# A two-layer encoder on one core: phases that end with one barrier and without GpSimd's drain, on two sets of semaphores

## The chip, the cores and the metric

The kernel runs on one core of one Trainium2 chip. The metric is the device time of one execution in microseconds, smaller is better. A core has five engines with queues of their own: TensorE (PE; its weight loads are PEld), VectorE (DVE), ScalarE (ACT), GpSimd (POOL) and SyncE (SP), and 16 DMA engines that all of them share. Engines wait for each other on semaphores only. A name with a q behind it (POOLq, SPq) is the engine's sequencer, where drains, semaphore instructions and DMA issues are shown.

## The reference

What is computed is an encoder trunk of two layers on one sequence of 1024 tokens of width 1024, in float32. Cut to its structure:

```python
def reference(x, ...):
    for layer in range(2):
        hn = rms_norm(x, mix_norm[layer])
        if layer == 0:
            u = hn @ ev_w_in
            y_att = diff_attention(u[..., :1536], ...)   # 4 heads, two softmaxes subtracted
            y_hy = hyena_mixer(u[..., 1536:], ...)       # long convolution through an FFT
            y = concatenate([y_att, y_hy]) @ ev_w_out
        else:
            u = hn @ od_w_in
            y = mlstm_mixer(u, ...) @ od_w_out           # chunkwise scan, forward and backward
        x = x + y
        x = x + hier_moe(rms_norm(x, ffn_norm[layer]), ...)
    return x

def hier_moe(x, ...):
    # top 1 of 4 groups, then top 2 of 8 experts inside it; tokens sorted by expert,
    # padded to blocks of 128, each block through its expert:
    hid = silu(xe @ w1[e]) * (xe @ w3[e])
    y = hid @ w2[e]
    # rows scaled by their gates and summed back per token
```

## The kernel before, in words

The program is a chain of 13 phases, run strictly one behind the other. In order they are: the attention projection (block at line 243), attention (533), the Hyena projection (1330), the Hyena filter (1548), the Hyena transform (1703), output projection and router of layer 0 (811), the experts of layer 0 (1976), the values of the mLSTM (2411), its gates (2627), its queries and keys (2828), its scan (2965), output projection and router of layer 1 (811 again) and the experts of layer 1 (1976 again). One block behind these, at the end of `build`, is only built when phases are cut off, and is not part of the program here.

A phase is one `nc.Block`: in it each engine has its own instruction list, and within a phase engines meet on semaphores written out by hand. `take(n)` hands a phase its semaphores: the first n of one pool of 46. Every phase counts from zero on the same ones. Semaphores that live across phases (those of the weight ring, `chunk_in`; of the gathered rows, `gather_in`; of the scattered rows, `given`; and some more) are allocated beside the pool and never cleared.

When a block closes, every engine drains (waits for its own instructions) and all engines meet at a barrier; GpSimd's drain is among these. `end_phase` (lines 110 to 113) then runs `nc.all_engine_barrier(sems_to_clear=pool_range)`: a further drain of every engine, a meeting at GpSimd, the clear of the pool's 46 semaphores by GpSimd, and a release of all engines. A phase is thus followed by two barriers, and the next phase's first instruction comes behind both.

What crosses the seams: SP loads weights into a ring of three slots of 2 MB (`load_chunk`, line 172), always three chunks ahead; `refill` and the loops of the expert phase issue them as slots come free, so that the first chunks of a phase are issued in the phase before. The router phase ends with two indirect gathers by GpSimd (line 867), which fetch the rows of the first two experts into `xg`, and VectorE's gates of the slots (lines 1278 and 1279).

In an expert phase GpSimd issues the indirect DMAs: `fetch` gathers the rows of expert e (line 2035), `give` adds the results of expert e to the output rows (line 2050), one more gather for an overflow block (line 2068), and for each further overflow block a gather (2086) and an adding scatter (2094), of which layer 1 has one here and layer 0 none. Before its list ends GpSimd waits for the last of the `give` transfers (line 2077), for `put` (line 1933) and for the last gather (line 2100). ScalarE casts each weight half to its high part (line 2228, the phase's first ScalarE work), VectorE takes the rest (2292), TensorE transposes the gathered rows (2131) and multiplies (2114 to 2122).

The values phase behind the experts of layer 0 begins on SP with loads of the residual rows just written, `x_ml` from `x_scratch` (line 2418), a broadcast gain, and further rows. ScalarE squares the rows (line 2494), VectorE normalises them (2562), TensorE turns them (2440) and multiplies (206 to 208). TensorE starts with 44 filler products (`idle_products`, line 201) before the first turn.

In the Hyena transform GpSimd multiplies eight pieces of `yT` in place (line 1893, counted on `added`); in the scan it adds the backward results onto the forward ones (line 3085, counted on `added_ok`). Nothing in those phases waits for the last of these counts: the drain at the block's end covers them.

Of the kernel before, what the change touches and what calls it, by code (L numbers as in the profile page):

```python
# [76 lines left out]
def build(nc, I, out):  # L77
    ctx = ExitStack()
    with ctx:
        POOL = 46  # L80
        pool = [nc.alloc_semaphore(f"phase_sem{i}") for i in range(POOL)]
        pool_range = range(pool[0].num, pool[0].num + POOL)
        chunk_in = [nc.alloc_semaphore(f"chunk_in{i}") for i in range(RING)]
# [11 lines left out]
        phases = [0]  # L95
# [14 lines left out]
        def end_phase():  # L110

            nc.all_engine_barrier(sems_to_clear=pool_range)
            phases[0] += 1

        def sb(stack, name, shape, dt=F32, side=None):
            return stack.enter_context(nc.sbuf_tensor(name, shape, dt, side=side))
# [95 lines left out]
        def attention_project(q, kH, kL, v, src, gain):  # L212
# [5 lines left out]
            with ExitStack() as st:  # L218
# [23 lines left out]

                with nc.Block() as block:
                    @block.sync
# [265 lines left out]
        def attention(q, kH, kL, v, o):  # L510
            (scored, max_neg, expd, comb, turned_lo, turned_hi, wt_lo, wt_hi, summed, o_copied, lam_in, lam_ok,
             chain, q_high, q_rest) = take(15)
            with ExitStack() as st:
# [18 lines left out]

                with nc.Block() as block:
                    @block.sync
# [162 lines left out]
        def out_route(name, yT, hs, head_gain, s0, xsrc, xdst, layer, slots, slot_gate, ctrl, xg):  # L697
# [6 lines left out]
            with ExitStack() as st:  # L704
# [105 lines left out]

                with nc.Block() as block:
                    @block.sync
# [471 lines left out]
        def hyena_project(z, yT, xnH, o, gain, post, hidden, consts):  # L1284
# [4 lines left out]
            with ExitStack() as st:  # L1289
# [39 lines left out]

                with nc.Block() as block:  # L1330
                    @block.sync
# [204 lines left out]
        def hyena_filter(z, zT, hidden, consts, hs, hd, hinv, tab):  # L1536
# [4 lines left out]
            with ExitStack() as st:  # L1541
# [5 lines left out]
                SUM = 6  # L1547
                with nc.Block() as block:
                    @block.sync
# [105 lines left out]
        def hyena_transform(z, zT, both, tab, hinv, yT):  # L1655
# [4 lines left out]
            with ExitStack() as st:  # L1660
# [7 lines left out]
                UNITS = 2 * FT  # L1668
# [31 lines left out]
                def result_of(c, i):  # L1700
                    return (KR if c else G)[:, 2 * i:2 * i + 2, :]

                with nc.Block() as block:
                    @block.sync
                    def _(sp):
                        sp.dma_start(skip[:], I["hy_skip"]).then_inc(skip_in, 16)
                        sp.wait_ge(done, forward_order(1, 0) + 4)
                        for kt in range(FT):
                            sp.dma_start(both[:, 8 * kt:8 * kt + 8, 0:CH], I["c_idft"][kt]).then_inc(inv_in[kt], 16)
# [177 lines left out]
                    @block.gpsimd  # L1887
                    def _(pool_e):
                        for n in range(2 * 4):
                            c, i = divmod(n, 4)  # L1890
                            g = times(yT[:, 4 + 2 * c + i // 2, :], i % 2)
                            pool_e.wait_ge(scaled, n + 1)
                            nc.gpsimd.tensor_tensor(g, g, result_of(c, i), ALU.mult).then_inc(added, 1)
                end_phase()


        @phase
        def experts(layer, slots, slot_gate, ctrl, total, xg, y, yidx, oidx, w_over):
# [9 lines left out]
            with ExitStack() as st:  # L1908
# [66 lines left out]

                with nc.Block() as block:
                    @block.sync
# [374 lines left out]
                for c in range(3):  # L2352
                    n = s0 + 3 * NE + c
# [26 lines left out]
        def ml_values(vA, xnH, src, gain):  # L2380
# [4 lines left out]
            with ExitStack() as st:  # L2385
# [24 lines left out]

                with nc.Block() as block:
                    @block.sync
# [185 lines left out]
        def ml_gates(xnH, cols, colb, apr, so, qkH):  # L2598
# [5 lines left out]
            with ExitStack() as st:  # L2604
# [21 lines left out]

                with nc.Block() as block:
                    @block.sync
# [176 lines left out]
        def ml_project_qk(qkT, xnH, wH):  # L2805

            (proj, padded, convolved, silued, weights_in, edges, chain, w_high, w_rest, first_half, lower) = take(11)
            with ExitStack() as st:
# [18 lines left out]

                with nc.Block() as block:
                    @block.sync
# [101 lines left out]
        def ml_scan(qkT, kn, vA, cols, colb, apr, hs):  # L2931
# [3 lines left out]
            with ExitStack() as st:  # L2935
# [9 lines left out]
                UNITS = NT * 2 * MH  # L2945
# [5 lines left out]
                FIRST = UNITS // 2  # L2951
# [12 lines left out]

                with nc.Block() as block:
                    @block.sync
# [110 lines left out]
                    @block.gpsimd  # L3077
                    def _(pool_e):
                        def add(u):
                            c, d, h, gi, n, col = unit(u)  # L3080
                            dst = hs[:, n, h * MV:(h + 1) * MV]
                            if u == FIRST:
                                pool_e.wait_ge(h_ok, FIRST)
                            pool_e.wait_ge(scaled_ok, u - FIRST + 1)
                            nc.gpsimd.tensor_tensor(dst, dst, num[:, u % 4, 0:MV], ALU.add).then_inc(added_ok, 1)

                        pool_e.wait_ge(k_lo, NT // 2)
                        pool_e.wait_ge(k_hi, NT // 2)
                        for u in range(UNITS):
                            if u < STATED:  # L3090
                                c, d, h, gi, n, col = unit(u)
                                if u >= 2:
                                    pool_e.wait_ge(cc_ok, u - 1)
                                nc.gpsimd.tensor_scalar(kw[:, u % 2, :], kn[:, n, h * P:(h + 1) * P], col(3), None,
                                                        ALU.mult).then_inc(kw_ok, 1)
                            if u - 4 >= FIRST:
                                add(u - 4)
                        for u in range(UNITS - 4, UNITS):
                            add(u)

                    @block.vector
# [134 lines left out]
        if phases[0] >= LAST_PHASE[0]:  # L3236
            with nc.Block() as block:
                @block.sync
                def _(sp):
                    for n in range(RING):  # L3240
                        sp.wait_ge(chunk_in[n], 16 * issued[n])
# [107 lines left out]
```

## Time and profile before

| | us |
|---|---|
| median of 3 runs | 2589.49 (2587.01 to 2590.59) |
| profiled execution: span from first to last instruction | 2584.1 |
| profiled execution: a time of its own beside the span | none is shown |
| TensorE busy | 2384.6 (92%) |
| VectorE busy | 1817.3 (70%) |
| ScalarE busy | 1457.0 (56%) |
| GpSimd busy | 472.1 (18%) |
| instructions | 32457 |

The page of the profile gives the busy time of each engine over the whole span. Drains, semaphore instructions and DMA issues do not count as busy; they stand in the view by source line, with their durations and the time of the first and the last start. The timeline gives starts to a hundredth of a microsecond, with the idle time before an instruction and what ended it in square brackets. The DMA view of a stretch gives the busy share (in tenths) and the GB/s of the DMA engines in 40 equal columns.

### The profile page before, as it was taken

To read this page: it belongs to the slowest core of one execution; us is meant where nothing else is said; L and a number is where in the kernel's file an instruction comes from. 1 tells how busy PE (TensorE), PEld (TensorE's weight loads), DVE (VectorE), ACT (ScalarE), POOL (GpSimd) and SP (SyncE) were. 2 spreads that over 40 slices of the span, in tenths; PEclk is the share of its full clock that TensorE was granted. 3 is DMA by queue.
4 is the path that set the end of the run, shared out by engine and by line. 5 is a ranking of instruction groups with operands and counts; after the bars stand their busy time and mean duration, and the time that the engine had idled before them with its cause. 6 is when DMAs were issued, how large, how long until landed. Compare 5 with 4: busy or idle time off the path is not lost. (4 is left out here: it accounts for less than half of the span.)

```text
span 2584.1 us, 32457 instructions
## 1 busy us (share of the span) xinstructions
PE 2384.6 (92%) x11594; PEld 1956.3 (76%) x11594; DVE 1817.3 (70%) x2055; ACT 1457.0 (56%) x1782; POOL 472.1 (18%) x433
## 2 busy tenths in 40 slices
PE   8989999796978999999996999997997999999996
PEld 7768877485867888888885877875775888888884
DVE  7848856568457998989883141478647899888982
ACT  6438842322216787888873241267424788887881
POOL 0001100102002333333320000026001233332321
PEclk9999999898988999999998999999997999999998
DMA  5110011111337999999995022012435999999996
GB/s 180 53 48 2 2 41 45 73 33 30 114 130 272 380 393 371 390 388 382 385 379 201 17 95 102 33 50 76 166 128 208 376 374 383 370 395 380 392 386 238
DMA packets 94377, 546.55 MB, mean 212 GB/s; under 512 B 19260, under 2 KB 31133, under 8 KB 68294
## 3 DMA queue, kind: packets, MB, share of 16 engines
q1 hardware_dynamic: 72822, 507.16, 50.3%
q0 software_dynamic: 19008, 33.61, 5.4%
q10 hardware_dynamic: 2448, 4.46, 0.5%
q8 instruction: 62, 1.02, 0.2%
q14 instruction: 37, 0.30, 0.0%
HBM read 525.72 MB, written 55.08 MB: 225 GB/s over the span
## 5 line engine op out<-in xcount | busy, mean ns | idle before, releaser
L2292 DVE TENSOR_TENSOR wL<-ring,wH 128x2048 fp32r<-128x2048 f32 x384 | 869.4, 2288 | 135.4 <-ACT wH L2228 129.4
L2228 ACT CAST wH<-ring 128x2048 fp32r<-128x2048 f32 x384 | 729.9, 1911 | 200.4 <-DMA ring<-in_moe_w 147.6
L2114 PE MATMUL psum<-wH,xgH 128*128 128x512 f32 x1024 | 407.1, 398 | 13.1 <-DVE xgL L2292 13.1
L2116 PE MATMUL psum<-wH,xgL 128*128 128x512 f32 x1024 | 400.9, 392 | 0.0
L2122 PE MATMUL psum<-wL,xgH 128*128 128x512 f32 x1024 | 275.2, 391 | 0.0
L2114 PEld LDWEIGHTS psum<-wH,xgH 128*128 128x128 f32 x1024 | 193.5, 189 | 54.7 <-DVE xgL L2292 13.3
L2122 PEld LDWEIGHTS psum<-wL,xgH 128*128 128x128 f32 x1024 | 192.8, 188 | 40.5
L2116 PEld LDWEIGHTS psum<-wH,xgL 128*128 128x128 f32 x1024 | 193.6, 189 | 38.5
L2114 PE MATMUL psum<-wH,hidH 128*128 128x512 f32 x512 | 206.0, 402 | 3.4 <-DVE hidL L2292 3.4
L2116 PE MATMUL psum<-wH,hidL 128*128 128x512 f32 x512 | 200.2, 391 | 0.0
L2032 POOL COPY gidx<-slots 128x1 int32 (+1 forms) x60 | 58.1, 968 | 496.4 <-PE psum L2131 496.4
L2122 PE MATMUL psum<-wL,hidH 128*128 128x512 f32 x512 | 137.7, 391 | 0.0
L208 PE MATMUL psum<-xn_high,ring_rest 128*128 128x512 f32 x320 | 126.6, 396 | 0.0
L2114 PEld LDWEIGHTS psum<-wH,hidH 128*128 128x128 f32 x512 | 96.5, 189 | 22.6 <-DVE hidL L2292 3.8
L206 PE MATMUL psum<-w_high_route_rest,y_high_route 128*128 128x512 f32 x256 | 104.0, 406 | 9.4 <-DVE ring_rest L196 8.9
L2122 PEld LDWEIGHTS psum<-wL,hidH 128*128 128x128 f32 x512 | 96.7, 189 | 20.2
L2116 PEld LDWEIGHTS psum<-wH,hidL 128*128 128x128 f32 x512 | 96.7, 189 | 18.3
L208 PE MATMUL psum<-w_high_route_rest,y_rest_route 128*128 128x512 f32 x256 | 101.0, 394 | 0.0
L207 PE MATMUL psum<-ring_rest,y_high_route 128*128 128x512 f32 x256 | 100.9, 394 | 0.0
L207 PE MATMUL psum<-ring_rest,xn_high 128*128 128x512 f32 x256 | 100.8, 394 | 0.0
L2046 POOL COPY yidx<-slots 128x1 int32 (+1 forms) x64 | 88.0, 1374 | 64.6 <-DMA out<-y,yidx 33.4
L629 DVE TENSOR_REDUCE neg_max<-psum 128x1 f32<-128x1024 f32 x64 | 75.4, 1220 | 29.2 <-PE psum L553 29.2
(436 smaller groups left out, 4622.2 us busy)
## 6 DMA issues: line engine op xcount, KB each, us to landing
ring<-in_moe_w SPq DMA_DIRECT2D x192, 2048.0 KB, 9.5
ring<-in_ev_w_in SPq DMA_DIRECT2D x6, 2048.0 KB, 10.1
xnT<-in_moe_w SPq DMA_DIRECT2D x6, 2048.0 KB, 15.2
ring<-in_od_w_in SPq DMA_DIRECT2D x6, 2048.0 KB, 15.5
xn_scratch<-xn_route SPq DMA_DIRECT2D x16, 512.0 KB, 2.6
ow<-in_moe_w SPq DMA_DIRECT2D x3, 2048.0 KB, 24.0
v_att<-in_x SPq DMA_DIRECT2D x8, 512.0 KB, 4.5
ring<-in_ev_w_out SPq DMA_DIRECT2D x2, 2048.0 KB, 7.8
```

Of the source, the lines that this page charges most:

```text
L206: nc.tensor.matmul(dst, lhs[0], rhs[0], start=start, stop=False)
L207: nc.tensor.matmul(dst, lhs[0], rhs[1], start=False, stop=False)
L208: return nc.tensor.matmul(dst, lhs[1], rhs[0], start=False, stop=stop)
L629: nc.vector.tensor_reduce(nmx[:, i % 2, c:c + 1], pair(u), AX, ALU.max, negate=True).then_inc(max_neg, 1)
L2032: nc.gpsimd.tensor_copy(idx[:, b:b + 1], slots[:, bass.ds(e, 1)]).then_inc(idx_ok, 1)
L2046: nc.gpsimd.tensor_copy(yidx[:, b:b + 1], slots[:, bass.ds(e, 1)]).then_inc(yidx_ok, 1)
L2114: nc.tensor.matmul(psum[:, bank, :], xh[:, k, :], w3[0][:, n, cols], start=(half == 0 and n == 0), stop=False)
L2116: nc.tensor.matmul(psum[:, bank, :], xl[:, k, :], w3[0][:, n, cols], start=False, stop=False)
L2122: ins = nc.tensor.matmul(psum[:, bank, :], xh[:, k, :], w3[1][:, n, cols], start=False, stop=(half == 1 and n == len(ks) - 1))
L2228: nc.scalar.copy(half_of(wH, b, e, c, half), raw(e, c, half)).then_inc(w_high, 1)
L2292: return nc.vector.tensor_tensor(out, whole, high.bitcast(F32), ALU.subtract)
```

## The change

Each block is opened with `no_gpsimd_drain=True`: at its end the other four engines drain, GpSimd does not, and the engines meet at a barrier of semaphores only. There are two pools of 46 semaphores, used in turn by the phases. `end_phase` has no barrier any more: GpSimd alone clears the pool of the phase that has just ended, while the others go on into the next block, which counts on the other pool. At the end of the transform and of the scan, GpSimd now waits for its own last additions by semaphore.

```diff
@@ build
-        pool = [nc.alloc_semaphore(f"phase_sem{i}") for i in range(POOL)]
-        pool_range = range(pool[0].num, pool[0].num + POOL)
+        sets = [[nc.alloc_semaphore(f"phase_sem{n}_{i}") for i in range(POOL)] for n in range(2)]
+        pool = list(sets[0])
...
         def end_phase():
 
-            nc.all_engine_barrier(sems_to_clear=pool_range)
+            first = pool[0].num
+            nc.gpsimd.sem_clear(range(first, first + POOL))
             phases[0] += 1
+            pool[:] = sets[phases[0] % 2]
...
@@ every block (lines 243, 533, 811, 1330, 1548, 1703, 1976, 2411, 2627, 2828, 2965, 3237)
-                with nc.Block() as block:
+                with nc.Block(no_gpsimd_drain=True) as block:
...
@@ Hyena transform, end of GpSimd's list
                             nc.gpsimd.tensor_tensor(g, g, result_of(c, i), ALU.mult).then_inc(added, 1)
+                        pool_e.wait_ge(added, 2 * 4)
...
@@ scan, end of GpSimd's list
                         for u in range(UNITS - 4, UNITS):
                             add(u)
+                        pool_e.wait_ge(added_ok, UNITS - FIRST)
```

## Rows read from the trace of the kernel before

**Rows 1.** The page of the kernel before: the span.

```profile
span 2584.1 us, 32457 instructions
```

**Rows 2.** Source view, line 243: operation, count, ns min/median/max, first and last start.

```profile
L243 ACTq DRAIN  x1: 614/614/614, 170.5 to 170.5; - x1
...
L243 SPq EVENT_SEMAPHORE  x1: 17/17/17, 171.2 to 171.2; - x1
```

**Rows 3.** Source view of line 112, the barrier in end_phase; columns as above.

```profile
L112 POOLq EVENT_SEMAPHORE  x26: 17/17/17, 171.5 to 2584.0; - x26
L112 POOLq DRAIN  x13: 34/40/41, 171.3 to 2583.5; - x13
...
L112 POOLq EVENT_SEMAPHORE_RANGE_CLEAR  x13: 283/283/287, 171.5 to 2583.7; - x13
L112 SPq EVENT_SEMAPHORE  x13: 17/17/17, 171.9 to 2584.1; - x13
```

**Rows 4.** Timeline of the first seam: start, us, engine, line, operation; idle before.

```profile
171.98 1.28 ACT L661 ACT_TABLE_LOAD   x1 [0.92 <-PEq L112]
172.00 0.29 POOL L603 CAST q_high<-q_turned 128x128 fp32r<-128x128 f32 x1 [171.57 <-POOLq L112]
```

**Rows 5.** Source view of line 811, the block of the two router phases.

```profile
L811 POOLq DRAIN  x2: 5154/5408/5661, 775.8 to 1955.1; - x2
L811 DVEq DRAIN  x2: 235/236/237, 779.3 to 1958.6; - x2
```

**Rows 6.** Source view of line 1976, the block of the two expert phases.

```profile
L1976 SPq DRAIN  x2: 7/7/7, 1368.9 to 2578.0; - x2
L1976 POOLq DRAIN  x2: 5199/5280/5362, 1376.4 to 2577.9; - x2
```

**Rows 7.** Source view of line 1703, the block of the Hyena transform.

```profile
L1703 POOLq DRAIN  x1: 2406/2406/2406, 634.5 to 634.5; - x1
```

**Rows 8.** Groups of POOL by line, with the number of indirect DMAs.

```profile
L2035 POOL DMA_INDIRECT xg<-xn_scratch,gidx x60 | 82.8, 1380 | 51.5 <-POOL gidx L2032 43.8 <-DMA x_scratch<-y,yidx 4.3 <-DMA out<-y,yidx 3.4
L2050 POOL DMA_INDIRECT x_scratch<-y,yidx x32 | 65.5, 2046 | 95.3 <-ACT y L2239 94.4 <-POOL yidx L2046 0.9
L2050 POOL DMA_INDIRECT out<-y,yidx x32 | 58.5, 1828 | 97.7 <-ACT y L2239 97.7
...
L867 POOL DMA_INDIRECT xg<-xn_scratch,slots x4 | 5.1, 1278 | 286.8 <-DVE slots L1266 286.1 <-issue 0.6
L2068 POOL DMA_INDIRECT xg<-xn_scratch,oidx x2 | 3.9, 1974 | 1.7 <-POOL oidx L2065 1.7
...
L2094 POOL DMA_INDIRECT out<-oy,oidx x1 | 1.6, 1577 | 17.0 <-DVE oy L2346 17.0
L2086 POOL DMA_INDIRECT xg<-xn_scratch,oidx x1 | 1.1, 1086 | 0.9 <-POOL oidx L2082 0.9
```

**Rows 9.** DMA view, 774 to 782 us: busy tenths, columns of 0.2 us.

```profile
DMA  0000000000000000009948821927994100000000
```

**Rows 10.** Timeline behind the two router seams.

```profile
781.83 1.90 ACT L2228 CAST wH<-ring 128x2048 fp32r<-128x2048 f32 x1 [22.35 <-PEq L112]
...
1961.68 1.90 ACT L2228 CAST wH<-ring 128x2048 fp32r<-128x2048 f32 x1 [22.82 <-PEq L112]
```

**Rows 11.** DMA view, 1376 to 1386 us: GB/s, columns of 0.25 us.

```profile
GB/s 418 418 393 418 401 410 401 393 385 393 393 377 352 311 295 238 197 188 139 131 90 41 25 25 25 25 25 8 0 98 213 197 229 459 344 295 344 262 295 197
```

**Rows 12.** Timeline of the values phase.

```profile
1386.02 1.06 ACT L2494 ACTIVATE sq_ml<-x_ml 128x1024 f32<-128x1024 f32 x1 [1.11 <-DMA x_ml<-x_scratch]
...
1390.81 1.09 PE L2440 MATMUL psum<-ident,x_ml 128*128 128x128 f32 x8 [1.45 <-DVE x_ml L2562]
```

**Rows 13.** A TensorE gap at a seam, and the granted clock behind it (column before DMA share).

```profile
483.28 2.10 PE L1564 MATMUL psum<-hy_w,hy_hidden 64*128 64x512 f32 x4 [5.51 <-PEq L112]
...
482.00:489.00 7.00, 5.72 (x16) 2.43 (x16) 2.08 (x4) 3.77 (x5) 0.00 (x0) 0.53 0.94 381
```

**Rows 14.** Source view of line 1334, a small transfer.

```profile
DMA to landing us min/median/max: 2.7/2.7/2.7
```

More of the change, by code:

```diff
@@ L531, in pair @@
                     return psum[:, b:b + 2, :].rearrange("p a b -> p (a b)")
-                with nc.Block() as block:
+                with nc.Block(no_gpsimd_drain=True) as block:
                     @block.sync
@@ L809, in y_source @@
                     return bank4(turn_bank(j, half))
-                with nc.Block() as block:
+                with nc.Block(no_gpsimd_drain=True) as block:
                     @block.sync
@@ L1328, in x_piece @@
                     return (slice(None), slice(4 * quad, 4 * quad + 4), slice(half * 512, (half + 1) * 512))
-                with nc.Block() as block:
+                with nc.Block(no_gpsimd_drain=True) as block:
                     @block.sync
@@ L1547, in hyena_filter @@
                 SUM = 6
-                with nc.Block() as block:
+                with nc.Block(no_gpsimd_drain=True) as block:
                     @block.sync
@@ L1701, in result_of @@
                     return (KR if c else G)[:, 2 * i:2 * i + 2, :]
-                with nc.Block() as block:
+                with nc.Block(no_gpsimd_drain=True) as block:
                     @block.sync
@@ L1974, in landed @@
                     return 16 * (n // RING + 1 + (0 if first(e) else e))
-                with nc.Block() as block:
+                with nc.Block(no_gpsimd_drain=True) as block:
                     @block.sync
@@ L2409, in turned @@
                     return psum[:, XT + half, :].rearrange("p (k t) -> p k t", k=4)
-                with nc.Block() as block:
+                with nc.Block(no_gpsimd_drain=True) as block:
                     @block.sync
@@ L2625, in chunked @@
                     return row.rearrange("g (c t) -> g c t", c=NT)
-                with nc.Block() as block:
+                with nc.Block(no_gpsimd_drain=True) as block:
                     @block.sync
@@ L2826, in block_of @@
                     return w(C0 + c)[:, :, ct * P:(ct + 1) * P]
-                with nc.Block() as block:
+                with nc.Block(no_gpsimd_drain=True) as block:
                     @block.sync
@@ L2963, in unit @@
                     return c, d, h, gi, n, col
-                with nc.Block() as block:
+                with nc.Block(no_gpsimd_drain=True) as block:
                     @block.sync
@@ L3236, in build @@
         if phases[0] >= LAST_PHASE[0]:
-            with nc.Block() as block:
+            with nc.Block(no_gpsimd_drain=True) as block:
                 @block.sync
```

## The prediction

> **What bounds the kernel now.** I read the page first. The span is 2584.1 us [rows 1], and the median of the three runs is 2589.49 us, so 5.4 us lie around the span. No other time of the profiled execution is shown; I make the sum against its span and add the 5.4 us. The page's busy shares say little here, since nothing in the interior of a phase changes: the change touches only the 13 phase ends. I therefore read the view by source line for the end barrier (line 112) and for the `nc.Block` line of each phase, then the timeline around each seam, then the DMA view where a transfer crosses one.
>
> Each phase now ends with two barriers. In the first, that of the block, every engine drains, GpSimd (POOL) collects and releases; SP is released at 171.2 at the first seam [rows 2]. The second, line 112, has a second set of drains, the clear of 46 semaphores (0.283 us) and a second release at 171.9 [rows 3]. ACT, the last to arrive (its drain ends at 170.5 + 0.61 = 171.1), starts its next work at 171.98 and POOL at 172.00 [rows 2, 4]. A seam so costs 0.9 us, about 0.65 of it for the second barrier (171.9 - 171.2, both to one decimal; the parts seen are the 0.28 us clear and three handshakes).
>
> **POOL's drain** is a separate cost in four phases. In the two router phases (line 811) it takes 5.15 and 5.66 us and ends at 781.0 and 1960.8, while VectorE's, the last of the others, ends at 779.3 + 0.24 = 779.5 and 1958.9 [rows 5]. In the two expert phases (line 1976) it takes 5.20 us from 1376.4 and 5.36 us from 2577.9 [rows 6], after a wait that has already seen every indirect transfer land. Where it has only POOL's arithmetic to wait for it ends with that arithmetic: 2.4 us on line 1703 [rows 7].
>
> What is the drain doing? POOL issued 60 + 32 + 32 + 4 + 2 + 1 + 1 = 132 indirect DMAs [rows 8]. The first expert phase has 30 + 32 + 1 = 63, the second two more (lines 2086 and 2094), 65. 5199/63 = 82.5 ns and 5362/65 = 82.5 ns: it looks like a walk over each DMA issued since the last drain. In the router phases, with two gathers each, the drain ends when the second gather has moved: its packets run to about 780.4 [rows 9]. The first gather's burst is over by 778.8, and that is the one that the first transposes of the expert phase need.
>
> **The change, part by part.**
>
> *Second barrier gone, eight plain seams.* I take 0.65 us each, 5.2 us. The new block end may use another barrier than the old one; the trace of before does not show it. Bounds: it costs the same (0.65 gained) or as much as both together (0 gained), and something a little cheaper is not excluded. I take the same, since the block end of before already has only semaphore instructions of 17 ns [rows 2].
>
> *Attention seam.* Here POOL's own cast is the first thing that TensorE waits for [rows 4], and the clear stays ahead of it in POOL's queue: 0.65 - 0.28 = 0.4 us. At the other seams the clear stands before POOL work that nobody waits for soon, such as the 1.8 us memset of the router phases; if that cover failed it would cost 0.28 us a seam.
>
> *Two router seams.* The next phase starts about 0.25 us after the last drain (at the first seam 0.1 us to the release, and from the second release to the first instruction 0.1 more [rows 2 to 4], rounded up). From 779.75 instead of 781.83, and from 1959.1 instead of 1961.68 [rows 10]: 2.1 + 2.6 = 4.7 us. ScalarE's cast of weights already loaded starts that phase, and SP's loads follow from it, so the whole phase should move with it.
>
> *Seam after the first expert phase.* Nominally 5.2 + 0.65 = 5.85 us. But the next phase begins with loads of x_ml from SP, and at 1376.4 the queue still holds weight loads: some 390 GB/s flow until 1379, then less, and a last engine runs at 25 GB/s up to 1382.75 [rows 11]. x_ml goes to all 16 engines; 32 KB on the last one at 25 GB/s is 1.3 us more, and half a microsecond goes by until it is seen (the gather's last packets fall in the column of 780.4, and the drain ends at 781.0 [rows 5, 9]): about 1384.6. Before, the square waited for this load to 1386.02 [rows 12]. So 1.4 us are left of 5.85; the rest is a stall of 4.4 us that changes its name to DMA. There is a second loss. TensorE's filler products start 5.7 us earlier and end earlier, and before the first transposes at 1390.81, preceded now by 1.45 us of idleness [rows 12], lie then 1.45 + 5.7 - 1.4 = 5.7 us. Around a gap of 5.5 us elsewhere the granted clock was 0.53 over 482 to 489 [rows 13], that is almost all at half speed, the 1.2 GHz level. Three microseconds of dense matmuls at that level lose 1.5 us. I take 0 for this seam, with -2 and +4 as the ends (clock fall twice as long; x_ml not queued behind the weights).
>
> *Last seam.* The drain of 5.36 us and the second barrier end the span at 2584.1. Afterwards the last drain of the others, at 2578.0 [rows 6], a release and the clear end it at about 2578.5: 5.6 us.
>
> *Added waits.* Two waits of POOL for its own last additions (lines 1893 and 3085) replace a drain that waited for the same instructions [rows 7]. Nothing is queued behind them on POOL but the barrier. 0, at most 0.1 us.
>
> Sum: 5.2 + 0.4 + 4.7 + 0 + 5.6 + 0 = 15.9 us. Span 2568.2, time 2573.6 us.
>
> **Forecast, 50%:** 2573.6 us. Its own range is 2570 to 2580: the barrier unknown (+5.6 if it gains nothing), the expert seam (-4 to +2), and some 2 us from clock grants that shift, mostly in our favour, since TensorE's gaps only get shorter elsewhere.
>
> **Rival 1, the walk is paid at the end, 34%.** Now no drain of GpSimd is left in the program. If whatever follows the span drains it, the walk comes there, over 132 DMAs if nothing has cleared them: 132 x 82.5 ns = 10.9 us, time 2584.5 us (24%). If only the last phase's share shows, 65 x 82.5 ns = 5.4 us, 2579.0 us (10%). For it: the drain of 0.04 us in line 112, right after the long one [rows 3], shows that the cost arises once and at whichever drain comes first. Against: the trace holds nothing behind 2584.1, so it doesn't show that a drain comes there at all. The Trainium skill ("Runtime: NRT & Kernel Launch", on the preamble and postamble) lists after the kernel a barrier, a semaphore reset and a DMA re-arm of about 1.5, 1.5 and 2 us; these fixed 5.0 us agree with the 5.4 us outside the span, and would leave the time at the forecast.
>
> **Rival 2, the seams were hiding something, slower, 6%.** When the second barrier and the drain go, each engine jumps into the next block at once, and its first instructions must be there. The second barrier gives such a fetch 0.65 us of cover. If none of it is prefetched, a start costs the time of a small transfer: 2.7 us from issue to landing on line 1334 [rows 14]. Twelve starts x 2.7 = 32 us against 15.9 gained: about 2606 us. The point from which it decides is (15.9 + 5.2)/12 = 1.8 us per start. Against: ACT arrived last at the first seam and started 0.9 us later, with the others, so there no fetch after arrival took more than 0.9 us. The Trainium skill (same page, "Instruction fetch mechanics") says that a taken branch outside the two loaded pages forces a fetch before execution can go on; it speaks against the change, and the equal starts at 171.98 and 172.00 do not bear it out.
>
> **Rival 3, the seams gain nothing but the drains, 10%.** The new barrier costs as much as the two, or every first instruction waits 0.65 us for code: 2579 to 2581 us.
>
> **How the numbers follow.** 0.2% is 5.2 us and about what a measurement of this kernel can tell from no change: faster is below 2584.3. The forecast, rival 3 and the small form of rival 1 lie there, 70%, and of the large form, which sits on the bound, I give less than half, 8%: 78% less some room for mishaps, 76%. Within 0.2%: 17%. Slower: 7%. The range is 2570 to 2585; it takes in the bounds of the forecast and both forms of rival 1, and leaves out rival 2.
>
> **What would show it.** Line by line in the new profile: no second group of drains; releases 0.65 us closer to the next start at plain seams; routers' first cast 0.25 us behind VectorE's last drain; in the values phase the wait of the first square for x_ml at over 4 us instead of 1.11, and the transposes hardly earlier; the span ending 0.5 us behind the last drain. If the span falls by 16 us and the time by 5, rival 1 holds. Starts that trail the release by more than 0.3 us are rival 2 or 3. I am wrong in the size of the expert seam if x_ml lands by 1381, and wrong about the walk if indirect DMAs late in the second expert phase get longer.

## The result, and the profile after

The changed kernel takes 2567.80 us (median of 6), the kernel before 2588.11 us in the same comparison; the ratio is 0.9921 with a 95% interval of 0.9906 to 0.9935. Two more comparisons gave 0.9938 (0.9926 to 0.9950) and 0.9929 (0.9913 to 0.9944). The three medians of the changed kernel lie within 0.4 us of each other, 2567.80, 2567.83 and 2567.42; those of the kernel before were 2588.11 (6 runs), 2584.91 (19), 2585.32 (11, in a comparison with other kernels) and 2585.77 (11), and the 2589.49 from which the prediction started (3). By the three ratios the gain is 16, 18 and 20 us, and the change is faster, as forecast. The forecast of 2573.6 us is 5.8 us too high, and the lower end of the range, 2570 us, lies 2.2 us above the measured time.

The page of the changed kernel, to be held against [rows 1]; both spans are of one execution each:

```profile
span 2566.7 us, 32355 instructions
...
PE 2384.4 (93%) x11594; PEld 1957.1 (76%) x11594; DVE 1817.5 (71%) x2055; ACT 1458.0 (57%) x1782; POOL 473.9 (18%) x433
```

The first seam in the source view of its block, now line 245, to be held against [rows 2]:

```profile
L245 SPq EVENT_SEMAPHORE  x2: 17/17/17, 173.5 to 173.7; - x2
...
L245 ACTq DRAIN  x1: 616/616/616, 172.9 to 172.9; - x1
```

ACT's drain ends at 172.9 + 0.62 = 173.5 and SP is released for good at 173.7. A first event of SP near its own drain at 173.5 is its arrival at the new barrier. There is no second group of drains, and of line 112's rows only the clear is left, on line 113, to be held against [rows 3]:

```profile
L113 POOLq EVENT_SEMAPHORE_RANGE_CLEAR  x13: 283/283/288, 173.7 to 2566.5; - x13
```

The timeline of the changed kernel at four seams (attention, the two routers, scan to router), to be held against [rows 4] and [rows 10]:

```profile
173.77 1.28 ACT L663 ACT_TABLE_LOAD   x1 [0.32 <-PEq L245]
...
174.12 0.29 POOL L605 CAST q_high<-q_turned 128x128 fp32r<-128x128 f32 x1 [173.69 <-POOLq L245]
...
778.02 0.20 DVE L1281 TENSOR_TENSOR slot_gate<-slot_gate,psum 128x48 f32<-128x48 f32 x1
778.58 1.90 ACT L2231 CAST wH<-ring 128x2048 fp32r<-128x2048 f32 x1 [20.32 <-PEq L813]
...
1948.32 1.36 PEld L2134 LDWEIGHTS psum<-ident,xg 128*128 128x128 f32 x7 [1.00 <-DMA xg<-xn_scratch,slots]
...
1948.60 1.90 ACT L2231 CAST wH<-ring 128x2048 fp32r<-128x2048 f32 x1 [20.59 <-PEq L813]
...
1789.67 1.32 POOL L3088 TENSOR_TENSOR xnT<-xnT,ml_num 128x256 f32<-128x256 f32 x2 [1.03 <-ACT ml_num L3057]
1791.67 0.33 SPq L828 DMA_DIRECT2D gate_route<-sigmoid_o_scratch  x1
```

The next phase starts at 173.77, 0.28 us behind ACT's drain. GpSimd follows 0.35 us later, at 174.12: that is the clear, in its queue before the cast. Behind the first router phase ScalarE starts at 778.58, behind the second TensorE at 1948.32 and ScalarE at 1948.60. VectorE's drain, the last one there, ends 0.31 us before the first of them, as its source view shows (starts 778.0 and 1947.8), to be held against [rows 5]; GpSimd's row is gone from it:

```profile
L813 DVEq DRAIN  x2: 237/237/237, 778.0 to 1947.8; - x2
```

At the scan's end GpSimd's last addition ends at 1791.0 and the router phase starts at 1791.67. In the expert phases, too, the long row of [rows 6] is gone and SP's drain is the last:

```profile
L1979 SPq DRAIN  x2: 7/7/7, 1362.5 to 2566.2; - x2
```

With the end of the last drain of the engines other than GpSimd, and the first instruction behind it, from such rows of all 13 phases, the seams are these (us; seams whose end GpSimd set before are marked):

```
seam behind              before  after  before, second profile
attention projection      0.87   0.28   0.87
attention                 0.87   0.29   0.87
Hyena projection          0.87   0.30   0.87
Hyena filter              0.87   0.30   0.87
transform (from GpSimd's
  last product)           0.94   0.41   0.94
router, layer 0 (*)       2.33   0.31   2.55
values                    0.88   0.37   0.88
gates                     0.87   0.28   0.87
queries and keys          0.87   0.28   0.87
scan (from GpSimd's
  last addition)          1.01   0.69   0.98
router, layer 1 (*)       2.81   0.31   2.96
experts, layer 1, to the
  end of the span (*)     6.07   0.53   6.08
```

Two engines start later than these seams say. At most seams an engine that waits for nothing else starts within 0.1 us of its release. But SP's first load of the gates phase comes 0.38 us behind it, and ScalarE's first cast of the experts of layer 1 (at 1948.60, above) 0.34 us, and both do so in all three profiles of the changed kernel. In both profiles of before the two come 0.06 and 0.07 us behind their release. SP's release and load after, and the load before, which the second barrier releases at 1500.38:

```profile
L2414 SPq EVENT_SEMAPHORE  x2: 17/17/17, 1488.7 to 1493.9; - x2
...
1494.29 0.36 SPq L2633 DMA_DIRECT2D gate_bias<-in_ml_gate_b  x1
...
1500.44 0.37 SPq L2630 DMA_DIRECT2D gate_bias<-in_ml_gate_b  x1
```

The seam behind the experts of layer 0 has to be read with the phase that follows. The timeline of the changed kernel from the start of the values phase to the first transposes, to be held against [rows 12]:

```profile
1370.75 0.34 SPq L2421 DMA_DIRECT2D x_ml<-x_scratch  x1
...
1370.80 7.25 PE L203 MATMUL psum<-ident 128*128 128x128 f32 x44 [13.35 <-PEq L1979]
...
1378.53 1.06 ACT L2497 ACTIVATE sq_ml<-x_ml 128x1024 f32<-128x1024 f32 x1 [5.34 <-DMA x_ml<-x_scratch]
...
1383.32 0.90 PE L2443 MATMUL psum<-ident,x_ml 128*128 128x128 f32 x3 [5.28 <-DVE x_ml L2565]
```

The first square now waits 5.34 us for x_ml instead of 1.11, and TensorE is idle for 5.28 us before its transposes instead of 1.45. What x_ml waits for is in the DMA view, 1370 to 1380 us in columns of 0.25 us, to be held against [rows 11]:

```profile
GB/s 418 401 393 393 426 410 401 393 385 385 401 344 410 393 393 410 418 385 418 401 393 459 344 492 401 410 467 377 426 377 393 410 410 426 410 372 423 454 405 328
```

The DMA engines move some 400 GB/s over the whole seam: the idle stretch of [rows 11], in which x_ml went before, is gone. And the windows view (PE, PEld, DVE, ACT and POOL busy, then the granted clock, DMA share, GB/s) shows what the gap did, to be held against [rows 13]:

```profile
1370.00:1375.00 5.00, 4.20 (x20) 4.23 (x21) 1.23 (x1) 2.42 (x3) 0.00 (x0) 0.50 1.05 399
...
1382.00:1389.00 7.00, 5.68 (x22) 5.20 (x23) 5.96 (x7) 4.86 (x9) 0.00 (x0) 0.52 0.24 79
1389.00:1393.00 4.00, 4.00 (x19) 3.28 (x18) 3.96 (x6) 2.60 (x3) 0.00 (x0) 0.99 0.00 0
```

After the gap the clock is 0.52, half speed, just while the first matmuls of the phase run, and back at 0.99 from 1389. From GpSimd's last wait in the expert phase to the last drain of the values phase it takes 123.3 and 122.9 us in two profiles of before, and 123.2, 121.8 and 122.9 us in three of the changed kernel: 0.5 us gained of 5.85, on the mean, where single profiles differ by more.

The same stretch in two parts shows what became of the rest (us; the end is that of TensorE's drain, the last one of the phase; the last column is the granted clock in the 6 us behind the start of the transposes):

```
                       last wait to      transposes to        clock
profile                transposes        the end              behind
before (2)             14.5, 14.2        108.7, 108.7         1.00, 1.00
changed kernel (3)     12.9, 11.9, 12.7  110.3, 109.9, 110.2  0.52, 0.59, 0.55
```

The transposes come 1.9 us earlier on the mean, and 1.4 us of that are lost behind them, where the clock is at half speed, or nearly so.

Elsewhere the shorter gaps helped the clock. Before, the windows view of the kernel before at the start of the scan:

```profile
1692.00:1696.00 4.00, 3.82 (x18) 3.85 (x19) 0.83 (x2) 1.17 (x2) 0.00 (x0) 0.50 0.32 73
1696.00:1700.00 4.00, 2.86 (x20) 2.46 (x18) 3.03 (x5) 2.78 (x5) 0.90 (x1) 0.88 0.64 190
```

and after, at the same point of the phase:

```profile
1682.00:1686.00 4.00, 3.02 (x15) 3.06 (x16) 0.69 (x1) 1.40 (x3) 0.00 (x0) 0.58 0.17 42
1686.00:1690.00 4.00, 2.83 (x23) 2.43 (x22) 3.20 (x5) 3.20 (x6) 0.93 (x1) 1.00 0.73 215
```

The stretch at half speed is some 3 us shorter. The scan's work takes 108.4 us in both profiles of before and 107.0 to 107.4 in three of the changed kernel, so 1.3 us are gained inside this phase.

### The profile page after: what moved, and what is told of

It is laid out like the page before. It is cut to its first block and busy times, and to the rows that moved or that the text cites. A ratio compares the mean times of both kernels' runs of the same rounds, so it can differ in the third digit from the quotient of the medians.

```text
span 2566.7 us, 32355 instructions
## 1 busy us (share of the span) xinstructions
PE 2384.4 (93%) x11594; PEld 1957.1 (76%) x11594; DVE 1817.5 (71%) x2055; ACT 1458.0 (57%) x1782; POOL 473.9 (18%) x433
## 5 line engine op out<-in xcount | busy, mean ns | idle before, releaser
L2242 ACT ACTIVATE y<-psum,slot_gate 128x1024 f32<-128x1024 f32 x64 | 71.5, 1117 | 44.7 <-PE psum L2125 44.6
```

The source lines that it names most:

```text
L2242: nc.scalar.activation(y[:, b, :], psum[:, 5:7, :].rearrange("p a b -> p (a b)"), ACT.Copy, scale=slot_gate[:, bass.ds(e, 1)]).then_inc(y_ ...
```

## The experiments

**The changed kernel again.** No edit.

> The changed kernel once more, beside the kernel before on the same chip. Theory (my sum of steps): each plain seam, from the last drain of the non-GpSimd engines to the next first instruction, is 0.28 to 0.31 us instead of 0.87, the two router seams 0.3 instead of 2.3 and 2.8, the last 0.2 instead of 5.4, and the values phase behind the experts gives the 5.3 us of its seam back; together 14 to 17 us of the time. Rival (something inside the phases got faster too): 20 us as the first medians say, and the Hyena transform phase (116.4 us of work in the first profile against 120.9 before) and the experts of layer 0 (583.9 against 587.1) are short again. If these two vary from run to run, they are noise and not the change.

Ratio 0.9938 (0.9926 to 0.9950), 16 us; the medians, 2567.83 against 2584.91 us, lie 17 us apart. The seams repeat the table within 0.01 us. The transform's work is 120.65 us here and 116.4 in the first profile, the experts of layer 0 584.7 and 583.9: phases scatter by some 4 us inside, whatever the kernel. For the transform the profiles show what goes with it: where it takes 120.7 or 120.9 us (this profile and the first of before) the granted clock is 0.51 and 0.50 over 6 us at 543 and 547, and where it takes 116.3 to 116.6 us (the other three) it is 1.00 there.

**The kernel before again.** No edit.

> The kernel before once more, for a second profile of it. Theory (differences inside phases are noise): the Hyena transform's work, 120.9 us in the first profile of before and 116.4 and 120.7 in the two of the changed kernel, takes either value here; the seams repeat to 0.02 us (0.87 at plain seams, 5.2 and 5.4 of drain in the expert phases). Rival: all of before's profiles lie at the long values and the change shortens phases inside. It also tells what lies outside the span: the run's time less its span, 2.1 us in every run of the changed kernel, and not the 5.4 us that I took from the median.

```profile
span 2582.9 us, 32457 instructions
...
L1976 POOLq DRAIN  x2: 5199/5280/5362, 1373.6 to 2576.6; - x2
```

These are the page's span and the expert phases' drains in this second profile of the kernel before. The run took 2584.84 us, so 1.9 us lie outside its span, not 5.4. The other executions of the kernel before say the same: over the 41 of the three later comparisons the time less the span is 1.8 to 3.1 us, and its median 1.9 to 2.1. The transform took 116.64 us, the value that I had seen only with the changed kernel; the drains are the same to the nanosecond. The change does not shorten that phase.

**Only the second barrier taken away.**

```diff
-                with nc.Block(no_gpsimd_drain=True) as block:
+                with nc.Block() as block:
```

(in all blocks of the changed kernel)

> Two pools and no second barrier, but every block ends with GpSimd's drain as before. Theory: the 12 seams lose the second barrier's 0.6 us each and the end 0.3, so 7.5 us of the time are gained; GpSimd's drains stay at 5.2 us (layer 0) and 5.4 us (layer 1) in the expert phases and end with the second gather in the routers. With the time outside the span unchanged, about 0.9971 of the time before. Rival, that the second barrier alone explains more than the drain: 12 us or more.

```profile
L1979 POOLq DRAIN  x2: 5211/5291/5371, 1371.1 to 2569.1; - x2
```

Ratio 0.9977 (0.9964 to 0.9990), 5.9 us gained where 7.5 were expected, which the interval (2.6 to 9.3 us) takes in. The plain seams are 0.22 to 0.24 us here, the drains in the source view of the expert block are whole. The second barrier is about a third of the gain. SP's late start is at another seam in this kernel, 0.40 us behind its release at the queries and keys.

**Only the block's drain taken away.**

```diff
-                with nc.Block() as block:
+                with nc.Block(no_gpsimd_drain=True) as block:
```

(in all blocks of the kernel before; `end_phase` keeps its barrier)

> Blocks end without GpSimd's drain, but line 112's barrier with its own drain of every engine stays, on one pool. Theory (any drain of GpSimd walks over all indirect DMAs since the last one, 82.5 ns each): GpSimd's drain on line 112, 0.04 us before, takes 5.2 us and 5.36 us behind the two expert phases, and in the router phases ends with the second gather; the time is that of before within 1.5 us. Rival (only the block's own drain is of the costly kind): line 112's drains stay at 0.04 us and 8 to 10 us are gained.

```profile
L112 POOLq DRAIN  x13: 34/46/5372, 173.3 to 2574.8; - x13
...
L112 POOLq EVENT_SEMAPHORE_RANGE_CLEAR  x13: 283/283/288, 173.6 to 2580.3; - x13
```

Ratio 0.9993 (0.9982 to 1.0004). The source view of line 112 shows where the cost went: its drain, at most 41 ns in [rows 3], takes 5.37 us behind the experts of layer 1. Either drain of GpSimd pays, and the first one pays all. The flag alone brings nothing measurable; it is worth something only if no other drain of GpSimd follows. The plain seams are 0.93 us here against 0.87, as they are 0.29 in the changed kernel against 0.23 with the old block end: the new block end costs 0.06 us more than the old one, and the second barrier 0.64 us, both times. A late start is here too, with both barriers in place: SP's first load behind the transform comes 0.47 us after its release.

**A drain behind everything.**

```diff
         moe(1, out, *lists1)
+        nc.gpsimd.drain()
```

> The changed kernel with one drain of GpSimd behind the last clear, and nothing else. Theory (walk over every indirect DMA since the last drain, nothing else clears them): the drain takes 132 x 82.5 ns = 10.9 us, and the time is 10.9 us above the changed kernel's. Rival 1 of the prediction (something behind the span drained GpSimd anyway): the span grows by 10.9 us but the time does not, since it moves from outside into the span. Rival (a ring of limited depth, or cleaning as the DMAs are issued): the drain takes 5.4 us or less.

```profile
L3240 POOLq DRAIN  x1: 5875/5875/5875, 2565.0 to 2565.0; - x1
```

5.88 us and not 10.9. The drain starts at 2565.0 and ends the span at 2570.9. The median is 2572.30 us, 4.5 above the changed kernel's in the same comparison. What lies outside the span is 2.1 to 2.2 us in the six executions with the drain and 2.0 to 2.2 us in the six without: the drain adds to the span and nothing behind it gets shorter, so nothing there was doing this work. Rival 1 falls with that. But my size for it, 132 times 82.5 ns, falls too.

**Drains inside the expert phases**, each behind waits for the scatters issued so far:

```diff
                                 give(e % 2, e - 4)
+                        pool_e.wait_ge(given, gave + 32)
+                        pool_e.wait_ge(got[1], got_base[1] + 16 * 3)
+                        nc.gpsimd.drain()
                         with pool_e.Fori(3, NE // 2) as i:
...
+                        pool_e.wait_ge(given, gave + 16 * (NE - 4))
+                        nc.gpsimd.drain()
                         pool_e.wait_ge(x_hi, NE - 1)
...
                         pool_e.wait_ge(given, gave + 16 * NE)
+                        nc.gpsimd.drain()
```

> The changed kernel with three drains of GpSimd in each expert phase, each behind waits that have seen the scatters land: before the loop over experts (8 indirect DMAs since the start in layer 0: 2 gathers of the router, 4 gathers, 2 scatters), behind the loop (52 more), and behind the last wait (5 more). Theory (82.5 ns for each DMA since the last drain): 0.7, 4.3 and 0.5 us in both layers. Rival (a cost of some 5 us per drain with the queue once used in a loop, whatever the count): the last two take 5 us each. The drains lie in GpSimd's idle time, so that the block end is cheap and the time stays within 1 us of the changed kernel's.

```profile
L2065 POOLq DRAIN  x2: 716/716/717, 854.2 to 2023.9; - x2
...
L2071 POOLq DRAIN  x2: 4297/4297/4297, 1314.0 to 2488.9; - x2
...
L2086 POOLq DRAIN  x2: 446/446/446, 1372.7 to 2543.8; - x2
```

0.72, 4.30 and 0.45 us in both layers, for 8, 52 and 5 indirect DMAs. With 5.20 us for 63 and 5.36 us for 65 this is 34 ns and 82 ns for each (for the 8 that gives 0.69 us, a little less than was measured). The single run took 2574.3 us, 6.5 us more than the changed kernel and not within 1 us of it. A part of that stood before any of these drains: the first phase ended 0.6 to 3.0 us later than in the three profiles of the changed kernel. The rest I can't assign.

**How much is left at most.** One drain after 8 DMAs and one at the very end, 124 later:

```diff
                                 give(e % 2, e - 4)
+                        if layer == 0:
+                            pool_e.wait_ge(given, gave + 32)
+                            pool_e.wait_ge(got[1], got_base[1] + 16 * 3)
+                            nc.gpsimd.drain()
...
         moe(1, out, *lists1)
+        nc.gpsimd.drain()
```

> The changed kernel with one drain of GpSimd behind the first 8 indirect DMAs of the program and one behind the last clear, 124 DMAs later. The law so far is 34 ns and 82 ns for each DMA since the last drain (5 to 65 DMAs); over all 132 it was 5.87 us, worth 71 DMAs. Theory (entries are cleaned as new ones need their place, so that never more than some 71 are left): the first drain takes 0.7 us and the last 5.87 us again. Rival (a store of fixed size is cleaned whole when it is full, so that the rest depends on the count): the last drain differs by 8 entries, 5.2 or 6.5 us, or by more.

```profile
L2066 POOLq DRAIN  x1: 711/711/711, 850.8 to 850.8; - x1
...
L3244 POOLq DRAIN  x1: 5866/5866/5866, 2563.2 to 2563.2; - x1
```

0.71 and 5.87 us. The last drain is the same for 124 and for 132 DMAs, and it is worth (5.87 - 0.03)/0.082 = 71 of them. No more than about 71 were left to walk over. That older ones are cleaned as new ones come is the reading that fits, but it is not shown: a walk that stops at a fixed number would look the same, and the work of cleaning was not seen anywhere. The median gather by GpSimd takes 1.06 to 1.07 us in both expert phases of all three profiles of the changed kernel, so no 82 ns are added to it in the second.

**The third weight chunk behind x_ml.** In the changed kernel, the load of chunk S_ML + 2 moves from the end of the first expert phase into the values phase:

```diff
-                            if s0 + 3 * NE + c - 1 < S_END:
-                                load_chunk(sp, s0 + 3 * NE + c - 1)
+                            n = s0 + 3 * NE + c - 1
+                            if n < S_END and n != S_ML + 2:
+                                load_chunk(sp, n)
...
                         sp.dma_start(gw[:], I["ml_gate_w"]).then_inc(gates_in, 16)
+                        load_chunk(sp, S_ML + 2)
                         for j in range(3, NT):
```

> The changed kernel, but the third weight chunk of the mLSTM is issued in the values phase behind its first loads of x_ml and of the gate weights, and no longer at the end of the expert phase of layer 0, so that 2 MB less stand in the queue ahead of x_ml. Theory (5.3 us of the seam were given back to the queued weights): the wait of the first square for x_ml falls from 5.34 to about 1.5 us, TensorE's gap before the first transposes from 5.3 to 1.5 us, and the clock does not fall behind it; the time is 4 to 6 us below the changed kernel's 2567.8. Rival (x_ml is slow for another reason, such as the scatters written just before): the wait stays above 4 us and the time within 1 us.

Its timeline at the first square and the first transposes, and its windows view behind them:

```profile
1372.02 1.06 ACT L2499 ACTIVATE sq_ml<-x_ml 128x1024 f32<-128x1024 f32 x1 [0.87 <-DMA x_ml<-x_scratch]
...
1376.82 1.09 PE L2445 MATMUL psum<-ident,x_ml 128*128 128x128 f32 x8 [1.62 <-DVE x_ml L2567]
```

```profile
1373.00:1380.00 7.00, 4.47 (x38) 3.98 (x36) 5.97 (x8) 5.58 (x11) 0.00 (x0) 1.00 1.02 395
1380.00:1384.00 4.00, 4.00 (x19) 3.26 (x18) 3.66 (x6) 4.00 (x6) 0.00 (x0) 1.00 0.95 361
```

The wait for x_ml is 0.87 us, TensorE's gap 1.62 us and the clock stays up. The median is 2562.3 us, the ratio to the kernel before 0.9912 (0.9898 to 0.9926): 5.5 us below the changed kernel's 2567.8. From GpSimd's last wait to the end of the values phase it takes 117.1 us instead of 121.8 to 123.2: the transposes come 8.4 us behind that wait, and the 108.7 us of before follow. The weights queued in front were what held x_ml.

**The same once more.**

> The version with the third weight chunk issued behind x_ml once more, beside the changed kernel on the same chip. Theory: 5 to 6 us below it again, about 0.991 to 0.992 of before, with the wait for x_ml at 0.9 us. Rival: the first 5.5 us were partly luck, and 2 us are left.

2561.80 us and 0.9907 (0.9890 to 0.9924), beside 2567.42 us for the changed kernel on the same chip: 5.6 us, with the wait at 0.66 us.

**More filler for TensorE.**

```diff
-                        idle_products(3, 44)
+                        idle_products(3, 76)
```

> The changed kernel with 76 instead of 44 filler products at the start of the values phase behind the experts, so that TensorE is busy until shortly before its first transposes while the wait for x_ml stays. Theory (the gap of 5.3 us costs the clock, 6.8 us at half speed from 1382): the granted clock stays at its upper level there, and the values phase takes 1.5 us less than the 121.5 to 122.9 us of the changed kernel; the time falls by about that, hardly to be told from noise. Rival (ScalarE and VectorE pace the phase's start, not TensorE): the clock stays up and the phase is no shorter.

```profile
1377.19 1.06 ACT L2497 ACTIVATE sq_ml<-x_ml 128x1024 f32<-128x1024 f32 x1 [5.16 <-DMA x_ml<-x_scratch]
...
1381.99 1.09 PE L2443 MATMUL psum<-ident,x_ml 128*128 128x128 f32 x8 [1.86 <-DVE x_ml L2565]
```

```profile
1380.00:1387.00 7.00, 4.23 (x27) 3.53 (x26) 6.66 (x10) 5.59 (x10) 0.00 (x0) 1.00 0.23 83
```

Timeline and windows: the wait for x_ml is still 5.16 us, the gap only 1.86 us, and the clock 1.00 where the changed kernel had 0.52. The values phase's work is 121.1 us, against 122.9, 121.5 and 122.6 in the three profiles of the changed kernel. These whole-phase times mix the clock with x_ml's wait, which is 5.34, 4.38 and 5.21 us in those three. From the first transposes to the end of the phase there is no such mix:

```
                                TensorE's gap before   transposes to the end
before (2), late chunk (2),
  more filler, one barrier,
  block's drain alone           0.4 to 1.9             108.7
drains after 8 and 124          3.9                    109.0
changed kernel (3), drain at
  the end, drains inside        5.2 to 5.8             109.8 to 110.3
```

With the filler the changed kernel's phase takes the 108.7 us of before. (In the run with drains after 8 and 124 DMAs x_ml came sooner, with a wait of 3.21 us, and the gap and the loss are smaller.) The clock's part is therefore 1.1 to 1.6 us, 1.4 on the mean of the three profiles of the changed kernel, and the rival (ScalarE and VectorE pace the start, and the phase is no shorter) falls. The time, 2567.38 us and 0.9937 (0.9919 to 0.9956), can't tell this gain from nothing.

**The changed kernel a third time.**

> The changed kernel a third time against the kernel before. Theory (the steps add up to 15 to 17 us; the 20 us of the first comparison were a high sample of before): 0.9935 with 0.992 to 0.995. Rival (20 us are real): 0.992.

0.9929 (0.9913 to 0.9944): between the two theories. The three ratios average to 0.9929, 18 us.

## Why the prediction was right, and where it was wrong

*The plain seams* were taken at 0.65 us each. They gained 0.57 to 0.59 at five of the eight, 0.51 behind the values, 0.53 behind the transform and 0.3 behind the scan: 4.3 instead of 5.2 us. The second barrier was worth the 0.65 us (0.64 measured), but the new block end costs 0.06 us more than the old one. Transform and scan are the two places with an added wait of GpSimd, which I had put at 0 to 0.1 us; behind the scan it comes to some 0.25 us. Behind the values SP, which led before, is the engine that starts late.

*The attention seam* was taken at 0.4 us and gained 0.28: from ACT's last drain to TensorE's first product it was 1.79 and is 1.51 us, and the clear takes 0.35 of the 0.59.

*The routers* gained 2.0 and 2.5 us to the first instruction, 4.5 together where 4.7 was forecast; to ScalarE's cast, from which I had reckoned, the second gained 2.2. The walk reading was right, with 82 ns for each DMA and 34 ns before, and shown by drains of five sizes, 5 to 65 DMAs.

*The expert seam* was taken at 0 and gained 0.5. Both halves of the step happened: x_ml behind queued weights (a wait "over 4 us", measured 5.34; moving the weights took it away) and the clock fall behind TensorE's gap (5.28 us, forecast 5.7). The two sizes nearly cancel, as forecast: the transposes come 1.9 us earlier (forecast 1.4) and the clock takes 1.4 us back (forecast 1.5).

*The last seam* was taken at 5.6 and gained 5.5 us.

*Clock luck* was put at some 2 us in the forecast's range and not into the sum. One part of it may be no luck: TensorE's gap before the scan got shorter in every profile, and the scan with it, by 1.3 us. Another is luck: the gates phase takes 97.1 us in both profiles of before, and 95.6, 97.2 and 95.6 us in the three of the changed kernel. In the three that take some 97 us the granted clock is 0.57 over 4 us, starting 2 to 3 us into the phase, and in the two of 95.6 us it is 1.00 there; on the mean that is 1.0 us.

In sum 4.3 + 0.3 + 4.5 + 0.5 + 5.5 + 1.3 = 16.4 us against 15.9 forecast, and with the gates phase 17.4; 16 to 20 were measured. The difference is smaller than the scatter of single phases.

*What failed* is the step from the span to the time. I set the profiled execution's 2584.1 us beside the median of 2589.49 and read the difference as 5.4 us "around the span". The second profile of before has 1.9 us outside, the 41 later executions of before 1.8 to 3.1, and the three profiled runs of the changed kernel 2.1 to 2.2. The rest of the 5.4 us was the distance between one execution and a median of three that lies some 4 us above the medians of 11 and 19 runs. This one term is 3.3 of the 5.8 us by which the forecast is off. The other 2.5 are the span (2568.2 forecast, 2566.7 measured) and the 1.0 us by which that execution lies above the median of the six. With 2 us outside, the same span of 2568.2 gives 2570.2 us, and a range moved down by 3.4 us holds the result. The mechanism and its terms held; this term, which no row showed, was mis-sized. The fixed 5.0 us of the Trainium skill ("Runtime: NRT & Kernel Launch", on the preamble and postamble), which I had found in agreement, do not agree with the 1.9 to 2.2 us measured; whether this metric takes them in at all, no run here shows. The warning stood in the times shown before: with three runs between 2587.01 and 2590.59 and a span of 2584.1, the profiled execution need not have been one of them.

*Rival 1* did not happen: the time outside the span is 2.0 to 2.2 us with and without a drain put at the end, no more than the 1.8 to 3.1 us of the kernel before. Its large form was mis-sized as well (5.9 and not 10.9 us). *Rival 2* did not happen at its price of 2.7 us at each of twelve starts, but its sign was there: two starts that nothing else holds trail their release by 0.38 and 0.34 us, above the 0.3 us that I had named, in every profile of the changed kernel and in none of before. Together they cost well under 1 us. The second barrier does not keep them away in general, since the kernel with both barriers and no drain has one too. What holds them is in no row. The Trainium skill's rule on taken branches (same page, "Instruction fetch mechanics") would fit, and so would other causes; no run here tells them apart. *Rival 3*: the new block end costs 0.06 us more than the old one, and not the 0.65 that would have taken the gain away.

## What to carry to other kernels

A seam is worth what ends last in it, together with what the next phase asks first: removing 5.85 us of barrier and drain in front of a load brought 0.5 us, and some 5.5 us more when one 2 MB chunk of prefetched weights was issued behind that load and no longer ahead of it. Leave the drain of GpSimd out everywhere or nowhere, since the next one pays for the indirect DMAs that were issued since the last. And before a time is predicted from a span, know both for the same execution; a median of three runs here was 4 us away from that of many.

## What the hardware showed that I had not expected

A drain of GpSimd whose indirect DMAs have all landed takes 34 ns and 82 ns for each such DMA since the last drain (5, 8, 52, 63 and 65 of them: 0.45, 0.72, 4.30, 5.20, 5.36 us), but no more than 5.87 us, for 124 as for 132. A drain that comes while the last gather is still moving ends some 0.1 us behind its landing. A TensorE gap of 5.3 us was followed by a granted clock of 0.52 over 1382 to 1389, where gaps of 1.6 and 1.9 us at the same place were followed by 1.00; the phase behind it took 1.4 us more, and the same 108.7 us to 0.02 in all seven profiles in which the gap was at most 1.9 us. And a start behind a barrier can come 0.3 to 0.4 us late for no reason that the profile shows, at the same place in every profile of a kernel.
